# Six gathered-row buffers in place of eight, nine weight chunks held in place of seven, and a later weighted row

## What is computed

```python
def peer_ffn(x, w_q, sub_keys, u, v):
    def chunk(xc):                                   # 128 tokens
        q = (xc @ w_q).reshape(TOKEN_CHUNK, PEER_HEADS, 2, PEER_HALF)
        s = jnp.einsum('thpd,pkd->thpk', q, sub_keys)
        sv, si = lax.top_k(s, PEER_TOPK)             # 16 best of 128, for two halves
        cand = sv[:, :, 0, :, None] + sv[:, :, 1, None, :]
        cand_id = si[:, :, 0, :, None] * PEER_NKEYS + si[:, :, 1, None, :]
        cv, ci = lax.top_k(cand.reshape(TOKEN_CHUNK, PEER_HEADS, PEER_TOPK * PEER_TOPK), PEER_TOPK)
        eid = jnp.take_along_axis(cand_id.reshape(...), ci, axis=-1)
        g = jax.nn.softmax(cv, axis=-1)
        act = jax.nn.gelu(jnp.einsum('thkd,td->thk', u[eid], xc))
        return jnp.einsum('thk,thkd->td', g * act, v[eid])
```

## Time and profile before

| | us |
|---|---|
| median of 3 runs | 1641.48 |
| lowest, highest | 1638.81, 1641.56 |
| the profiled execution, its own time | 1634.68 |
| its span | 1632.9 |
| mean granted TensorE clock | 0.904 of full |
| DMA bytes | 653.28 MB, 400 GB/s over the span |

### The profile page before, as it was taken

How to read it: one execution, slowest core, us unless ns; L and a number is a source line. 1 busy time by engine, 2 the same in 40 slices (tenths; PEclk the granted TensorE clock), 3 DMA queues, 4 the chain that set the end, 5 groups by cost and what they waited for, 6 DMA issues and landing times.

```text
span 1632.9 us, 15981 instructions
## 1 busy us (share of the span) xinstructions
PE 1220.4 (75%) x4534; PEld 724.9 (44%) x4534; DVE 1207.9 (74%) x2649; ACT 729.2 (45%) x2772; POOL 653.2 (40%) x516
## 2 busy tenths in 40 slices
PE   8987788867787688866687668887777766756554
PEld 7875355534454265533354326553444422222111
DVE  0035979887688887846768887877777999887776
ACT  2222634545544544424544363544454444445444
POOL 0002433445534333314544343333553444456552
PEclk9999999989889899987899899998989999897778
DMA  7749999999999999999999999999999999999996
GB/s 282 300 183 422 363 426 417 423 423 421 422 423 411 422 421 423 423 424 413 422 422 422 400 392 419 424 423 422 421 417 423 387 394 413 401 421 422 422 421 271
DMA packets 91961, 653.28 MB, mean 400 GB/s; under 512 B 10145, under 2 KB 11873, under 8 KB 12769
## 3 DMA queue, kind: packets, MB, share of 16 engines
q0 software_dynamic: 73728, 536.90, 79.8%
q1 hardware_dynamic: 18144, 115.36, 17.4%
HBM read 651.17 MB, written 1.05 MB: 399 GB/s over the span
## 4 chain that ended last, share of the span: by engine, by line
DMA 40%; DVE 31%; PE 10%; issue 9%; ACT 7%; POOL 2%; SPq 0%; DVEq 0%; POOLq 0%; ACTq 0%
DMA ring<-in_uv,expert 40%; DVE ring L854 10%; DVE xs L868 7%; PE bank L354 3%; PE bank L372 3%; PE ybank L513 2%; POOL ring L952 2%; DVE si L727 2%; DVE buf L721 1%; ACT wgt L680 1%; DVE buf L757 1%; DVE picked L760 1%; ACT half_p L668 1%; DVE ci L727 1%; DVE sv L724 1%
## 5 line engine op out<-in xcount | busy, mean ns | idle before, releaser
L952 POOL DMA_INDIRECT ring<-in_uv,expert x512 | 653.0, 1275 | 955.1 <-DVE xs L868 530.7
L513 PE MATMUL ybank<-ring,diag 128*128 128x512 f32 x1248 | 709.8, 706 | 388.9 <-ACT diag L691 388.5
L854 DVE SCALAR_TENSOR_TENSOR ring<-ring,tok 128x1024 f32<-128x1024 f32 x512 | 620.3, 1223 | 236.6 <-DMA ring<-in_uv,expert 229.8
L513 PEld LDWEIGHTS ybank<-ring,diag 128*128 128x128 f32 x1248 | 247.3, 214 | 764.0 <-ACT diag L691 532.2
L666 ACT ACTIVATE sq<-dots 128x2 f32<-128x2 f32 x256 | 52.1, 204 | 760.4 <-DVE ring L854 760.3
L868 DVE SCALAR_TENSOR_TENSOR xs<-ring,wgt,xs 128x1024 f32<-128x1024 f32 x200 | 256.4, 1282 | 61.3 <-ACT wgt L680 61.2
L354 PE MATMUL bank<-wring,hT 128*128 128x256 f32 x768 | 179.6, 390 | 0.0
L680 ACT ACTIVATE wgt<-th,half_p 128x1 f32<-128x1 f32 x512 | 170.1, 379 | 8.6
L372 PE MATMUL bank<-hT,wring 128*128 128x128 f32 x1408 | 170.0, 281 | 2.9 <-DVE tok L846 1.6
L372 PEld LDWEIGHTS bank<-hT,wring 128*128 128x128 f32 x1408 | 167.8, 198 | 9.4 <-issue 5.9
L354 PEld LDWEIGHTS bank<-wring,hT 128*128 128x128 f32 x768 | 151.7, 198 | 40.8 <-issue 20.7
(11 more groups left out here) (101 smaller groups left out, 711.4 us busy)
## 6 DMA issues: line engine op xcount, KB each, us to landing
wring<-in_chunks SPq DMA_DIRECT2D x92, 1024.0 KB, 9.1
held<-in_chunks SPq DMA_DIRECT2D x14, 1024.0 KB, 17.4
ring<-in_uv,expert POOLq DMA_INDIRECT x512, 12.5
xs<-in_x SPq DMA_DIRECT2D x2, 512.0 KB, 11.3
wpool<-in_w_pool SPq DMA_DIRECT2D x2, 512.0 KB, 13.1
trunk_out<-buf SPq DMA_DIRECT2D x4, 256.0 KB, 4.9
cst<-in_consts SPq DMA_DIRECT2D x1, 672.0 KB, 6.3
buf<-in_peer_keys SPq DMA_DIRECT2D x2, 128.0 KB
```

The source lines that it names most:

```text
L513: ins = pe.matmul(ybank[m][:, :], diag[:, nth % DIAGS, :], ring[:, (2 * t + r) % RING, D + m * BANK:D + (m + 1) * BANK], start=(nth == ten ...
L854: dve.scalar_tensor_tensor(out=ring[:, g % RING, 0:D], in0=ring[:, g % RING, 0:D], scalar=1.0, in1=tok[:, :], op0=ALU.mult, op1=ALU.mult, ...
L952: pool.indirect_dma_start(ring[:, g % RING, :], None, uv, bass.IndirectOffsetOnAxis(ap=expert[:, w % 2, at:at + 1], axis=0)).then_inc(row_ ...
```

## The change

Four edits:

1. `HELD` from 7 to 9: the second and third chunk of the queries' projection get buffers of their own too.
2. `RING` from 8 to 6. Two ring buffers of 16 KB a partition go, two held chunks of 8 KB come.
3. In VectorE's tick the weighted row of the tick before stands behind both dots, not between them.
4. The last window's searches take 7.5 ticks a head in place of 5.5. They end at tick 234 of the stream in place of 220. Since a tick with a search has both rows on TensorE, VectorE has 199 weighted rows in place of 200.

```diff
-HELD = 7
+HELD = 9
...
-RING = 8
+RING = 6
...
         def head_tick(w, h, step):
 
-            return when(w, 46 + 11 * h // 2 + 2 * step) if w else first_heads[h][step]
+            if w == 0:
+                return first_heads[h][step]
+            return when(w, 46 + (15 if w == windows - 1 else 11) * h // 2 + 2 * step)
...
             dot(dve, 2 * t)
+            dot(dve, 2 * t + 1)
             if t:
                 weighted(dve, t - 1)
-            dot(dve, 2 * t + 1)
```

## The result

The changed kernel is slower: 1886.57 us as the median of four runs, beside 1640.9 us for the kernel before. The ratio is 1.1494, with a 95% interval of 1.1461 to 1.1527. The forecast was slower, 1700 us in a range of 1648 to 1770; the sign came true and the size did not. The loss is about 245 us where 58 were forecast.

What follows compares the result with a forecast made beforehand. Gather and weight bytes at about 422 GB/s were taken as the bound. From the profiled 1634.7 us, -9.9 + 56 + 12 = +58 gave 1693; the three-run median's 6.8 us offset made it 1700 us, range 1648 to 1770.

Steps and rivals of the forecast that it cites:

- The loop: Six buffers and the later weighted row, priced together: a gather is left 4.7 us from issue to landing.
- the size of g: Time a gather needs with DMA engines nearly empty: taken as 5.8 us, between 4.7 (fastest weight load) and 6.3 (fastest gather).
- T = (5.2 + g)/2: Time of a two-row tick: 5.2 us from even dot to next issue plus the gather's g; forecast 5.5 us.
- rival (B): Deeper starvation: searches, softmax and gates delay issues, g acts like 7.2, T = 6.2; 1819 us at worst; chance 0.10.
- rows land every 4.97/2 = 2.49 us: In quiet ticks the odd row's dot was taken to start 2.49 us after the even row's.
- The term of +56 us: Cost over the 136 ticks without weights: 136 x 5.5 = 748 us, less the 691.8 they took before.
- Six buffers with the old order would leave 7.2 us: Aside in the pricing: time left a gather if only the ring shrank; "It is the pair that bites.".
- The ticks with weights: The 120 ticks where weight chunks run beside gathers: 0.1 us a tick lost to gathers meeting chunks, +12 us.
- Held chunks: Two more chunks held save four 1024 KB loads of 2.48 us each, -9.9 us, as long as bytes bound there.
- The searches: Thinning the last tile's searches: at most 7.2 us gained while bytes bound, 0 in a loop of 5.5 us.
- The signs: Marks expected in the changed profile: quiet slices near 380 GB/s, DMA share about 0.9, issue to landing 6 to 8 us.
- Rival A: The loop just fits: a gather needs no more than 4.7 us, bytes stay the bound, 1624 us; chance 0.10.

Runs made afterwards that it cites:

- e6_half_sum: The changed kernel with VectorE's weighted row over only 512 of the 1024 columns: 1842.5 us, ratio 1.1227.
- e13: The kernel before with seven ring buffers, eight held chunks and the weighted row behind both dots: 1697.2 us, ratio 1.0384.
- e1: The kernel before with six ring buffers in place of eight and nothing else: 1751.3 us, ratio 1.0666.
- m1_gathers_alone: Not the model: random 1 MB gathers at fixed numbers in flight, then the kernel's dot and weighted-row loop; six buffers, new order took 6.23 us a tick.
- x1_tensor_ticks_old: The changed kernel with the old searches' choice of last-window ticks that give both rows to TensorE: 1864.8 us, ratio 1.1401.
- m2_loops_and_loads: The bare gather loop with one 1 MB load a tick: 7.46 us (eight buffers, old order), 7.46 (six, old), 8.04 (six, new) a tick.
- e3_ring6_order: The kernel before with six ring buffers and the weighted row behind both dots, seven chunks held, old searches: 1871.2 us, ratio 1.1402.

## Why the prediction was wrong in size

- **The bound** (bytes at 422 GB/s, every gather issued as early as a buffer allows) was right, and so was the question put to each edit.
- **The loop** came true as a structure: the pair does it (+230), the order alone is free (-5), a shorter weighted row shows at once (e6_half_sum), and an equal allowance gives an equal quiet tick (e13 and e1).
- **The failed step is the size of g**, "I take g = 5.8". That is a good value for a gather by itself, 5.5 us in m1_gathers_alone, between the bounds given. In the loop a gather has others beside it, and the even row, the one whose g stands in T = (5.2 + g)/2, takes 6.9 us there. In the kernel, in x1_tensor_ticks_old (its trace has landing times and its first 178 ticks are the changed kernel's), the even rows of the quiet ticks from 370 to 470 us take 6.7 us on average and the odd ones 8.2. I had "g acts like 7.2" as a rival (B), for searches and gates; the quietest ticks come near it without any. Beside it, "rows land every 4.97/2 = 2.49 us" was carried over into a regime where it no longer holds: the odd row came up to 3.9 us behind in the piece shown, and so the 5.2 us are at times 6.6, and 5.5 on average in m1's loop. The term of +56 us measured +173.
- **The full rate while busy** was assumed silently: a bubble was counted as idle time, with 422 GB/s on both sides of it. In the changed kernel's quiet ticks the DMA share is 0.90 and the rate 326, that is 362 GB/s while busy in place of 418 (422/1.01). Of the 1.5 us that a quiet tick lost, 0.6 is idle time (0.1 x 6.4 us) and the rest, 0.9, slower movement.
- **"Six buffers with the old order would leave 7.2 us"** was put as harmless, on the strength of the shortest gather of 512, 6.3 us. It costs 110 us. A minimum over a trace tells what one gather can do, not what a loop of them gets.
- **The ticks with weights** (+12 us) took 84 us more than their bytes: +74 and the 10 us that fewer loads should have saved. The step that failed is "a chunk can use what the rows leave idle". m2_loops_and_loads shows 0.58 us a tick lost in the new order with a load in every tick, 70 us over 120 ticks. But in the kernel the two buffers cost there by themselves (840 us in e1_ring6 beside 800), and the new order adds 45 (885 in e3_ring6_order), while m2 has no loss with six buffers in the old order. What of the kernel makes that difference was not tried.
- **Held chunks** (-9.9 us): as bytes they are right, but bytes no longer bound the ticks in question. The prediction made this its condition ("as long as bytes bound") and then took it as met at 5.6 us a tick by bytes against a loop of 5.5; the loop was 6.4. What they brought is within the noise.
- **The searches** (0): some +15 us by the ratios, 7 us of it found in the ticks where the edit acts. The cause stays open; the choice of ticks with both rows on TensorE is the likeliest.
- **The signs.** Slices near 340 GB/s had been named as the mark of rival B, and that is what came; the total is above even B's 1819 us. GpSimd's wait for VectorE was to stay and grew from 531 to 930 us. The median from issue to landing, expected at 6 to 8 us, is 8.1 in x1_tensor_ticks_old.
- **Rival A** is decided by one number: a gather alone takes 5.5 us, not under 4.7. The Trainium skill ("DMA: Bandwidth & Descriptors", section "Anatomy of one DMA — SWDGE (gpsimd) path") fits such a DMA as 2.0 us and its bytes at 436 GB/s, an estimate of 4.4 us for 1 MB. The 5.5 us measured from GpSimd's issue are 1.1 us more, and the measurement decides.

## What to carry to other kernels

When a ring of buffers is made smaller, write down how long a transfer may take from issue to landing. Compare it with what the same transfer takes at the smallest number in flight that gives the full rate, not with the shortest one seen. Here that is three in flight and 7.2 us, and the allowance has to stand clear of it: in the quiet ticks 9.7 us was enough (5.0 us a tick), 7.2 us cost 0.6 us a tick and 4.7 us cost 1.4. An edit that releases a buffer later is free as long as the ring has room and very dear once it has none, so two such edits must be priced together and measured together. And look at which release comes first in a pair: giving VectorE the odd row in place of the even one was worth 99 us here with the same buffers and the same bytes.

## What the runs showed of the hardware

Random gathers of 1 MB (128 rows of 8 KB) need three in flight for the full 422 GB/s. With one it is 181 GB/s, with two 358 GB/s, and with two the DMA engines count as busy for 0.98 of the time: a busy share near 1 does not mean the full rate, so the GB/s beside it must be read too. From GpSimd's issue to landing it is 5.3 to 5.7 us with one in flight, 5.5 us as a median with two, 7.2 with three and 9.7 with four. Two gathers that were issued 1.8 us apart around a bubble (156 GB/s from 1760 to 1762 us) were dotted 3.9 us apart, where a full queue lands one every 2.5 us.
